# Attention of a two-layer decoder on one core: heads taken in pairs, values as the standing operand

## The reference, cut to what matters

```python
def dense_causal_attention(q, k, v):          # MLA: 96 query-key rows per head, 64 value columns
    logits = jnp.einsum('bqhd,bkhd->bhqk', qb, k).astype(jnp.float32) * scale
    logits = jnp.where(key_pos[None, :] <= q_pos[:, None], logits, -jnp.inf)
    p = jax.nn.softmax(logits, axis=-1).astype(v.dtype)
    return jnp.einsum('bhqk,bkhd->bqhd', p, v)
...
def dsa_branch(q, k, v, q_i, k_i, w_i, pos):  # DSA: 64 rows per head, top 64 keys per query
    ...
    logits = jnp.einsum('bqhd,bqnhd->bqhn', qb, k_sel).astype(jnp.float32) * scale
    logits = jnp.where(valid[:, :, None, :], logits, -jnp.inf)
    p = jax.nn.softmax(logits, axis=-1).astype(v.dtype)
    return jnp.einsum('bqhn,bqnhd->bqhd', p, v_sel)
...
    y_a = mla_branch(...) @ w_o_mla
    y_b = dsa_branch(...) @ w_o_dsa
    merged = g[..., :D_MODEL] * y_a + g[..., D_MODEL:] * y_b
    return merged @ w_out
```

## Time and profile before

| what | us |
|---|---|
| median of three executions | 1607.92 |
| span of the profiled execution | 1606.3 |
| PE busy in the span | 1584.2 |
| DVE busy | 1293.7 |
| ACT busy | 1025.3 |

### The profile page before, as it was taken

One profiled execution on the slowest core, in us unless ns is written; L12 is line 12 of the kernel. 1 busy time (PEld: TensorE's weight loads), 2 busy tenths in 40 slices (PEclk: granted clock), 3 DMA queues, 4 the chain that ended last, 5 costly groups with the idle time before them and its releaser, 6 DMA issues.

```text
span 1606.3 us, 19209 instructions
## 1 busy us (share of the span) xinstructions
PE 1584.2 (99%) x7629; PEld 1319.6 (82%) x7630; DVE 1293.7 (81%) x1307; ACT 1025.3 (64%) x950; POOL 57.0 (4%) x54
## 2 busy tenths in 40 slices
PE   8999999999999999999999999999999999999996
PEld 7888888888788888888888888888888888888885
DVE  6885765446697578999889889889888889888887
ACT  5656444444456645777777777777777777777773
POOL 0000000000000001000000100000100000100000
PEclk9999999999999999999999999999999999999998
DMA  9542466555444347999999999999999999999992
GB/s 348 183 144 89 152 210 209 184 189 178 155 158 132 129 160 257 352 374 327 373 375 357 365 378 325 373 376 357 374 377 319 376 365 365 376 367 334 369 372 82
DMA packets 230687, 453.13 MB, mean 282 GB/s; under 512 B 9920, under 2 KB 15552, under 8 KB 230592
## 3 DMA queue, kind: packets, MB, share of 16 engines
q1 hardware_dynamic: 228400, 447.60, 79.1%
q10 hardware_dynamic: 2192, 4.23, 0.8%
HBM read 450.75 MB, written 1.05 MB: 281 GB/s over the span
## 4 chain that ended last, share of the span: by engine, by line
PE 96%; DVE 2%; ACT 0%; issue 0%; DMA 0%; DVEq 0%
PE bank L1539 29%; PE bank L1541 29%; PE bank L1540 29%; PE bank L2020 4%; PE bank L1714 2%; PE bank L1933 1%; PE bank L1742 0%; PE bank L1743 0%; PE bank L1906 0%; PE bank L1907 0%; DVE split L445 0%; PE bank L1741 0%; DVE x L1254 0%; DVE xT L979 0%; DMA x<-x_dram 0%
## 5 line engine op out<-in xcount | busy, mean ns | idle before, releaser
L445 DVE TENSOR_TENSOR split<-raw,split 128x2048 fp32r<-128x2048 f32 x327 | 747.8, 2290 | 100.5 <-ACT split L440 99.7
L440 ACT CAST split<-raw 128x2048 fp32r<-128x2048 f32 x327 | 625.5, 1913 | 181.6 <-PE bank L1541 181.6
L1539 PE MATMUL bank<-split,xe_pair 128*128 128x512 f32 x784 | 309.8, 395 | 0.0
L1541 PE MATMUL bank<-split,xe_pair 128*128 128x512 f32 x784 | 305.9, 390 | 0.0
L1540 PE MATMUL bank<-split,xe_pair 128*128 128x512 f32 x784 | 305.3, 389 | 0.0
L429 DVE TENSOR_TENSOR split<-raw,split 128x2048 fp32r<-128x2048 f32 (+3 forms) x96 | 208.5, 2175 | 115.5 <-ACT split L423 114.9
L423 ACT CAST split<-raw 128x2048 fp32r<-128x2048 f32 (+3 forms) x96 | 174.5, 1818 | 167.2 <-PE bank L1541 165.6
L1539 PE MATMUL bank<-split,xT 128*128 128x512 f32 (+2 forms) x544 | 217.0, 399 | 2.6 <-DVE xT L979 1.2
L1541 PE MATMUL bank<-split,xT 128*128 128x512 f32 (+2 forms) x544 | 208.2, 383 | 0.0
L1540 PE MATMUL bank<-split,xT 128*128 128x512 f32 (+2 forms) x544 | 208.0, 382 | 0.0
L1539 PE MATMUL bank<-split,hT 128*128 128x512 f32 x488 | 190.6, 391 | 0.0
(11 more groups left out here) (248 smaller groups left out, 1597.8 us busy)
## 6 DMA issues: line engine op xcount, KB each, us to landing
raw<-moe_w_dram SPq DMA_DIRECT2D x330, 1024.0 KB, 6.4
raw<-w_in_dram SPq DMA_DIRECT2D x31, 1024.0 KB, 5.1
raw<-dense_w_dram SPq DMA_DIRECT2D x30, 1024.0 KB, 5.1
raw<-w_out_dram SPq DMA_DIRECT2D x8, 1024.0 KB, 5.1
early<-moe_w_dram SPq DMA_DIRECT2D x6, 1024.0 KB, 14.1
raw<-w_o_mla_dram SPq DMA_DIRECT2D x4, 1024.0 KB, 5.0
raw<-w_o_dsa_dram SPq DMA_DIRECT2D x4, 1024.0 KB, 5.1
raw<-w_in_dram SPq DMA_DIRECT2D x4, 912.0 KB, 5.3
```

The lines of the kernel that those rows point to most:

```text
L440: act.copy(split[:, n % SPLIT, HEAD, :], landing(n, j)[:, :]).then_inc(heads_made, 1)
L445: dve.tensor_tensor(split[:, n % SPLIT, REST, :], landing(n, j)[:, :], split[:, n % SPLIT, HEAD, :].bitcast(F32), ALU.subtract).then_inc(r ...
L1539: pe.matmul(out_, act_[REST], w[HEAD], start=first, stop=False)
L1541: return pe.matmul(out_, act_[HEAD], w[REST], start=False, stop=last)
```

## The change

Six things change together.

1. `qk` is split: MLA heads as before (`qk_mla`), DSA heads by pairs (`qk_dsa`): in each even step from 8 on both heads' products are issued, the one on array rows 0 to 63 into bank 4, the other on rows 64 to 127 into bank 5. The pair waits for the maxima of the unit just before it.
2. Value products go by pairs p = 0 to 7 (`pv_pair`): values stand (64 columns), turned probabilities move (256 and 128 columns), one head writes PSUM partitions 0 to 63 and the other 64 to 127 of the same bank. The output is so already turned. `pv_pair(i / 2 - 2)` stands first in each even step from 4 on.
3. The reciprocal sums of a pair (`pair_shares`, DVE) are spread over 64 columns each by ACT (`shares_spread`) and turned by PE as a fourth transpose of `turn_probs(u)` for u = 2p + 2 and 2p + 3; two more calls, u = 16 and 17, follow the loop.
4. `turned_probs` copies 512 columns where it copied 384, into four buffers where there were three.
5. `pair_normed` (DVE) multiplies each pair's output by the turned shares, `pair_head` (ACT) rounds it, `pair_rest` (DVE) makes the rest half. `norm_heads`, `heads_turn`, `heads_turned` and `heads_rest` go.
6. After the loop the order on ACT and DVE changes, and PE's waits before the output products.

The core of the diff:

```diff
@@ ACT
                 def turned_probs(u):
                     k = 16 * l + u
-                    act.wait_ge(p_tr, k + 1)
+                    lo = 0 if u < 16 else 384
+                    hi = W if u >= 2 else 384
+                    act.wait_ge(p_tr, 18 * l + u + 1)
                     if u >= NPT:
-                        act.wait_ge(pv_mm, k - NPT + 1)
-                    act.copy(pT[:, u % NPT, :], bank[6 + u % 2][:, 0:384]).then_inc(p_ev, 1)
...
+                        act.wait_ge(pv_mm, 16 * l + 2 * ((u - NPT) // 2) + 2)
+                    if u >= NPT + 2:
+                        act.wait_ge(o_ev, 8 * l + (u - NPT - 2) // 2 + 1)
+                    act.copy(pT[:, u % NPT, lo:hi], bank[6 + u % 2][:, lo:hi]).then_inc(p_ev, 1)
+
+                def shares_spread(p):
+                    act.wait_ge(shares, 8 * l + p + 1)
+                    if p >= 2:
+                        act.wait_ge(p_tr, 18 * l + 2 * p)
+                    act.copy(wide_of[p % 2].rearrange("p t (u d) -> p t u d", u=2),
+                             rden[:, :, 2 * p:2 * p + 2].unsqueeze(3).to_broadcast([P, T, 2, VDIM])).then_inc(shares_wide, 1)
+
+                def pair_head(p):
+                    act.wait_ge(o_ev, 8 * l + p + 1)
+                    act.copy(oT[:, HEAD, p // 4, p % 4, :], o_pair[p // 4][p % 4]).then_inc(oT_ev, 1)
 
                 for i in range(16 + 1):
                     if i < 16:
                         exps(i)
-                    else:
-                        heads_turned(0)
+                    if i >= 3 and i % 2:
+                        shares_spread((i - 3) // 2)
                     if i >= 1:
                         turned_probs(i - 1)
+                    if i >= 7 and i % 2:
+                        pair_head((i - 7) // 2)
...
+                shares_spread(7)
                 chunk_tile(8, 1)
+                pair_head(5)
+                pair_head(6)
+                for u in (16, 17):
+                    turned_probs(u)
                 head(23)
+                pair_head(7)
                 for h in range(2):
                     sigmoids(h, 0)
-                heads_turned(1)
@@ DVE
+                def pair_shares(p):
+                    dve.wait_ge(probs, 16 * l + 2 * p + 2)
+                    dve.reciprocal(rden[:, :, 2 * p:2 * p + 2], den[:, 2 * p:2 * p + 2, :].rearrange("p u t -> p t u")).then_inc(shares, 1)
+
+                def pair_normed(p):
+
+                    dve.wait_ge(pv_mm, 16 * l + 2 * p + 2)
+                    dve.wait_ge(p_ev, 18 * l + 2 * p + 4)
+                    dve.tensor_tensor(o_pair[p // 4][p % 4].rearrange("p (t s) -> p t s", t=T), blocks(bank[p % 2], T), share_of(p),
+                                      ALU.mult).then_inc(o_ev, 1)
+
+                def pair_rest(p):
+                    dve.wait_ge(oT_ev, 8 * l + p + 1)
+                    rest_of(dve, [oT[:, i, p // 4, p % 4, :] for i in (HEAD, REST)], o_pair[p // 4][p % 4], o_rest)
 
                 for u in range(16):
                     maxima(u)
+                    if u >= 2 and u % 2 == 0:
+                        pair_shares(u // 2 - 1)
+                    if u >= 6 and u % 2 == 0:
+                        pair_normed(u // 2 - 3)
+                    if u >= 8 and u % 2 == 0:
+                        pair_rest(u // 2 - 4)
@@ PE
+            def qk_dsa(u):
+
+                pe.wait_ge(row_max, 16 * l + u)
+                pair = (u - 8) // 2
+                for t in range(T):
+                    keys = (t + 1) * P
+                    for half in range(2):
+                        rows = slice(DH * half, DH * half + DH)
+                        ins = pe.matmul(bank[4 + half][:, t * P:t * P + keys], qTd[rows, pair, t * P:(t + 1) * P], kTd[rows, pair, 0:keys],
+                                        start=True, stop=True)
...
             def turn_probs(u):
...
+                    pe.wait_ge(p_ev, 18 * l + u - 1)
+                    pe.wait_ge(shares_wide, 8 * l + u // 2)
...
+                if u >= 2:
+                    ins = tp(bank[6 + u % 2][:, 384:W], wide_of[(u // 2 - 1) % 2][:, u % 2, :])
                 ins.then_inc(p_tr, 1)
...
+            def pv_pair(p):
+
+                m, pair, to = p // 4, p % 4, bank[p % 2]
+                pe.wait_ge(p_ev, 18 * l + 2 * p + 2)
...
+                if p >= 2:
+                    pe.wait_ge(o_ev, 8 * l + p - 1)
...
+                for half in range(2):
+                    u, h = 2 * p + half, 2 * pair + half
+                    rows = slice(VDIM * half, VDIM * half + VDIM)
+                    pe.matmul(to[rows, 0:SEQ], v(0, h), pT[:, u % NPT, 0:SEQ], start=True, stop=False)
+                    pe.matmul(to[rows, P:SEQ], v(1, h), pT[:, u % NPT, SEQ:3 * P], start=False, stop=True).then_inc(pv_mm, 1)
 
             f = 0
             for i in range(16 + 3):
+                if i >= 4 and i % 2 == 0:
+                    pv_pair(i // 2 - 2)
                 if i < 16:
                     qk(i)
...
-                if i >= 3:
-                    pv(i - 3)
...
             branch_tile("oa", 0, 0, 0)
+            for u in (16, 17):
+                turn_probs(u)
             branch_tile("oa", 0, 0, 1).then_inc(ya_mm, 1)
-            pe.wait_ge(proj_ev, base + T * NCH)
-            heads_turn(1)
+            pe.wait_ge(o_ev, 8 * (l + 1))
```

More of the change, by code:

```diff
@@ L220, in build @@
         score = fixed("score", [P, T, SEQ])
-        o_tok = [[proj[:, t, C_DQ + m * W:C_DQ + (m + 1) * W] for t in range(T)] for m in range(2)]
+        o_pair = [[proj[:, m, C_DQ + p * SEQ:C_DQ + (p + 1) * SEQ] for p in range(4)] for m in range(2)]
+        wide_of = [proj[:, :, C_Q + i * P:C_Q + (i + 1) * P] for i in range(2)]
         silu = put("silu", [P, T, W], r_proj)
@@ L279, in build @@
         c_rest, o_rest, m_rest, x_rest, h_rest, gat_rest, wr_ready = (
-            sem(n) for n in ("latents_rest", "heads_rest", "merged_rest", "x_rest", "hidden_rest", "gathered_rest", "router_split"))
+            sem(n) for n in ("latents_rest", "pair_rest", "merged_rest", "x_rest", "hidden_rest", "gathered_rest", "router_split"))
         consts = sem("consts_ready")
@@ L292, in build @@
         qk_mm, row_max, probs, p_tr, p_ev, pv_mm, o_ev = (
-            sem(n) for n in ("qk_mm", "row_max_ready", "probs_ready", "probs_turned", "probs_evacuated", "pv_mm", "heads_normed"))
-        o_tr, oT_ev, y_mm, merged, m_tr, m_ev, out_mm = (
-            sem(n) for n in ("heads_turned", "heads_evacuated", "branches_mm", "merged", "merged_turned", "merged_evacuated", "out_mm"))
+            sem(n) for n in ("qk_mm", "row_max_ready", "probs_ready", "probs_turned", "probs_evacuated", "pv_mm", "pair_normed"))
+        shares, shares_wide, oT_ev, y_mm, merged, m_tr, m_ev, out_mm = (
+            sem(n) for n in ("pair_shares_ready", "pair_shares_spread", "pair_head_ready", "branches_mm", "merged", "merged_turned", "merged_evacuated", "out_mm"))
         ln_var, ln_rstd, ln_done, x_tr, x_ev = (sem(n) for n in ("ln_variance", "ln_rstd", "ln_done", "x_turned", "x_evacuated"))
@@ L391, in proj_bank, with share_of @@
             return bank[(6 if c == ATT else 2) + t]
-        def heads_bank(m, t):
-            return bank[(2 if m else 4) + t]
+        def share_of(p):
+            first = (2 * p + 2) % NPT
+            return pT[:, first:first + 2, 384:W]
         def gate(l, h, t, b):
@@ L1468, in _ @@
                         rest(22)
[L1470 to L1473, removed]
                 def gate_mla(h):
@@ L1491, in merge @@
                         dve.tensor_tensor(ga, ga, gb, ALU.add).then_inc(merged, 1)
-                heads_rest(0)
-                norm_heads(1)
+                pair_shares(7)
+                pair_normed(5)
+                pair_rest(4)
+                pair_normed(6)
+                pair_rest(5)
+                pair_rest(6)
+                pair_normed(7)
                 rest(23)
+                pair_rest(7)
                 gate_mla(0)
-                heads_rest(1)
                 rest(24)
@@ L1708, in qk @@
                     keys = (t + 1) * P
-                    if u < 8:
-                        q, kk = qTm[:, h, t * P:(t + 1) * P], kTm[:, h, 0:keys]
-                    else:
-                        rows = slice(DH * (h % 2), DH * (h % 2) + DH)
-                        q, kk = qTd[rows, h // 2, t * P:(t + 1) * P], kTd[rows, h // 2, 0:keys]
-                    ins = pe.matmul(bank[4 + u % 2][:, t * P:t * P + keys], q, kk, start=True, stop=True)
-                ins.then_inc(qk_mm, 1)
+                    ins = pe.matmul(bank[4 + u % 2][:, t * P:t * P + keys], qTm[:, u, t * P:(t + 1) * P], kTm[:, u, 0:keys],
+                                    start=True, stop=True)
@@ new lines, in qk_mla @@
+                ins.then_inc(qk_mm, 1)
+            def qk_dsa(u):
[6 more added lines that the diff above has]
+                        ins = pe.matmul(bank[4 + half][:, t * P:t * P + keys], qTd[rows, pair, t * P:(t + 1) * P], kTd[rows, pair, 0:keys],
```

(10 more changed lines are left out.)

61 lines of the change are left out of this document (18 added, 43 removed).

## The result

The changed kernel takes 1614.16 us (median of six executions, 1611.45 to 1615.21), the kernel before 1609.49 in the same comparison (six, 1607.85 to 1609.98). The ratio, taken over all executions and given with its 95% interval, is 1.0033 [1.0023, 1.0043]: slower by a third of a per cent. The time lies in the predicted range, and the sign is the one given the largest chance; the size is not the predicted one, +4.7 us between the medians for +2.9. The profiled execution has a span of 1612.0, 5.7 more than that of before. Over all comparisons the executions of the kernel before lie in two groups, 1607.57 to 1608.16 and 1608.78 to 1610.13 us, and their median falls now into the one and now into the other, so differences under 2 us are read from the distances inside a layer further down and not from medians.

What follows compares the result with a forecast made beforehand. PE (TensorE), busy all through attention, was taken to bound the kernel. Per layer, 6.3 us saved against 7.7 of waits gave +1.4, +2.9 for two layers; 1607.9 + 2.9 = 1610.8 us, range 1605.5 to 1619.

Steps and rivals of the forecast that it cites:

- the sign: Whole kernel: slower given 0.50, within 0.2% 0.37, faster 0.13.
- the sum: Per layer: 6.3 us less PE work against 7.7 of new waits, +1.4 us.
- Gain 1: DSA query-key products, four pairs a layer: row halves run side by side, so a pair costs one head, not two.
- Gain 2: Value products: two heads share the time on column halves; a pair costs 1.06 us with two switches, against 1.22.
- rival B: Value pairs: column halves run one after the other, +4.8 us a layer, 1617.5 us; chance 0.22.
- Wait 1: PE before value pairs of steps 10 to 16 waits for ACT's copy, 0.7 to 1.1 us each, 3.9 a layer.
- Wait 2: Step 10: the query-key pair waits for the maxima of unit 9 on DVE, 0.7 us.
- Wait 3: Step 16: PE's transposes wait for ACT's spread copy of pair 6, 2.1 us.
- Wait 4: Merge after the loop: 0.5 us lost at the merged tile and 0.5 at the first output product.
- Rival C: Value pairs do not wait, 3.9 us a layer comes back: 1603.0 us; chance 0.14.
- A: The case as summed, whole kernel: 1610.8 us, own range 1606 to 1614.5; chance 0.60.
- rival D: PE clock in attention: waits of 2 us bring it to its lower level, 1614 us and more; chance 0.04.

Runs made afterwards that it cites:

- experiment 2: Changed kernel with eight dummy identity products on PE in the wait of step 16: 1610.09 us, ratio 1.0009 to the kernel before.
- experiment 6: Changed kernel with gate pieces ahead of value pairs in steps 10 to 16, unit 22's cast later, three more orders changed: 1598.71 us, ratio 0.9939.
- experiment 10: The version of experiment 6 with both heads of each value pair written through the same column half: 1606.98 us, ratio 0.9990.
- experiments 7: Changed kernel with its DSA query-key products put back to one head a step, the value part alone: 1618.54 us, ratio 1.0063.
- experiment 8: Changed kernel with gate pieces ahead of the value pairs of steps 10, 12 and 14 alone: 1608.77 us, ratio 1.0005.
- experiment 4: Changed kernel with gate pieces ahead of the value pairs of steps 10, 12, 14 and 16: 1605.52 us, ratio 0.9981.

## Why the prediction was right, and where it was not

**The sign and the mechanism.** Right, and for the reasons given: cheaper products, and waits that cost more. Without the clock (experiment 2) the layers are 1.16 and 1.12 us longer; the sum said 1.4. Removing the waits one by one turned the change from 1.0033 to 0.9939, so they, and the clock behind the longest of them, are the loss. The gain, too, comes out as summed: the version of experiment 6 is 4.4 to 4.6 us a layer shorter than before with 1.8 us of waits left, so 6.2 to 6.4 without them, against 6.3 in the sum.

**Gain 1** was right: 1.86 for value and query-key pair against 1.92, and 3.4 a layer for pairing alone. **Gain 2** was right in its choice of side by side: 0.81 from the start of a pair to the next product, and rival B, 0.22 of the chance, is excluded by that row and by experiment 10. The Trainium skill's ratio for three column tiles ("TensorE: Matmul & The Clock Gate", Measured speedup vs the span model) had made a pair 0.83 without its switches, where the row has 0.81 with the one behind it. In experiment 10 one head with the switch behind it takes 130.64 − 129.89 = 0.75, so the second head on its own half adds some 0.06; the trace doesn't agree with that estimate here, and two halves overlap nearly in full.

**Wait 1:** predicted 3.9 (0.7 to 1.1 each), in the profile 0.99, 1.14, 0.99 and 0.68, 3.8 together. **Wait 2:** 0.7 predicted, 0.47. **Wait 3:** 2.1 predicted, 2.19, with the chain as described. This is ACT in time, the changed kernel:

```profile
153.35 0.59 ACT L916 COPY pT<-bank 128x512 f32<-128x512 f32 x1
153.83 1.90 ACT L425 CAST split<-raw 128x2048 fp32r<-128x2048 f32 x1
155.63 0.40 ACT L902 ACTIVATE sm<-sm,mx 128x128 f32<-128x128 f32 x1
...
156.52 0.39 ACT L922 COPY proj<-rden 128x256 f32<-128x256 f32 x1
```

The copy of unit 13, the cast of unit 22, the exponentials of unit 15, and only then the spread copy that PE waits for. **Wait 4:** 0.5 and 0.5 predicted (0.9 in the sum), 0.34 and 0.24. Rival C is gone with wait 1. The single terms can't be added to the +1.1 to the tenth, since an idle time begins at the modelled end of the last pass and the filling behind it is in neither list. A's own range, 1606 to 1614.5, does not follow from its terms: the bounds of the waits alone, added up, reach from 1605.4 to 1616.4.

**The step that failed** is rival D: "In the rows it is 1.00 throughout; should the waits of 2 us bring it to the lower of its two levels for some us, each of these costs half its length. 1614 and more; little speaks for it." Its price was right, its chance of 0.04 was not: in the changed kernel the clock fell behind the wait of step 16 in both layers, at 1.5 to 1.6 us each, which is the larger part of the loss; the sum had the clock at nothing. It was also no rival of A but stood on top of it: A's waits were its cause. I had argued from attention stretches in which PE never waits, and these can't speak for or against what a wait does to the clock. That the time still lies in the range is in part luck: the range reached up to 1619 for the sake of rival B, and B did not happen. Of the 3.4 us between 1610.8 and 1614.16, 1.6 are the median of before, which came out higher than in the first three executions, and 1.8 the change.

**What stays open** is what decides a fall. Four profiled executions have the wait of 2.19 in both layers (the changed kernel twice, experiments 7 and 8); of these eight waits six were followed by a fall, and those in layer 1 of experiments 7 and 8 were not. By the clock of single microseconds the six falls began between some 1.0 us before the end of the wait and some 0.9 behind it. The 1.70 of experiment 4 was not followed by one, and the layer norm's 1.43 and 0.52 were in two of the twelve profiles (experiments 4 and 7). The Trainium skill ("TensorE: Matmul & The Clock Gate", Part 1, What's actually happening) says that the chip judges the engine's activity in stretches that run on by themselves and don't start with the kernel, so that the moment depends on where the work falls in them; the two layers of experiment 8 are compatible with that, and no run here tests it.

## What to carry to other kernels

A wait on the engine that bounds a kernel costs its length, and a clock that may fall behind it: price waits of 2 us with the clock on top, not as another case. When operands are turned so that a product needs a late copy, look at what stands ahead of that copy on its engine, however idle that engine is on average; moving one cast and four gate pieces a layer turned this change from a loss (ratio 1.0033) to a gain (0.9962). And before a change with several parts is dropped, time its parts alone: one of these was worth half a per cent on the first try.

## What the runs showed of the hardware

Two heads' float32 products on two column halves take 0.81 us where one column half takes 1.45. The granted clock fell to one half for some 3.4 us, once for some 6.9, behind waits of 2.19 us that in other executions or layers had no such effect, and twice behind waits of 1.43 and 0.52 us close together. Where the same wait was filled with 2.05 us of products of the identity, the clock fell in neither layer of the one profiled execution.
